# A two-layer trunk on one core: another order of the recurrence, and the one-token samples' new state made in the second feed-forward stage

## The chip, the cores and the metric

The kernel runs on one core of one Trainium2 chip. The metric is the device time of one execution in microseconds, from several runs. A profiled execution gives the trace. Engines are named as in the profile: PE is TensorE (matmuls, with their weight loads as PEld), DVE is VectorE, ACT is ScalarE, POOL is GpSimd, SP is SyncE, which here does nothing but issue DMAs.

## The reference

A trunk of two layers is run on a prompt of 256 tokens and, with its own states, on 8 samples of one token each. The kernel keeps them side by side: N = 264 columns, of which the first 256 are the prompt and the last 8 the samples. All is float32. A layer is:

```python
x = x + 0.5 * swiglu(rmsnorm(x, norm_ffn1), ffn1_w_in, ffn1_w_out)
h = rmsnorm(x, norm_mix); proj = h @ w_in
y_rwkv, shift, wkv = rwkv7_mix(...)      # 16 heads of 64
y_sc, sc_buf = short_conv_mix(...)
y_ssm, ssm_conv, ssm = mamba2_mix(...)
x = x + concatenate([y_rwkv, y_sc, y_ssm]) @ w_out
x = x + 0.5 * swiglu(rmsnorm(x, norm_ffn2), ffn2_w_in, ffn2_w_out)
```

The change is in rwkv7_mix. Per head, with a state S of 64 x 64, it does for each token

```python
Sa = einsum('bhij,bhj->bhi', S, -kk_t)
S = S * w_t[:, :, None, :] + Sa[..., None] * b_t[:, :, None, :] + v_t[..., None] * k_t[:, :, None, :]
y_t = einsum('bhij,bhj->bhi', S, r_t)
```

and then normalises y within each head (mean and variance over 64), scales it, adds a bonus and gates it. For a sample there is one token, an old state S read from memory (8 samples x 16 heads x 64 x 64) and a new state that is an output. For the prompt the kernel works in four chunks of 64 tokens, where each chunk needs the inverse of a triangular 64 x 64 matrix.

## The kernel before

A layer has two stages, "front" (first feed-forward, input projection, the two other mixers, the gates of this one) and "back" (the recurrence, the output product with w_out, the second feed-forward). Each engine has a list of its own, written out by hand, and works it in order; semaphores carry the dependences. So an instruction that waits holds all behind it on its engine.

**The recurrence.** Heads go in pairs: pair p is heads 2p and 2p+1, RT = 8 pairs. One loop over g = 0..9 overlaps three ages of pairs: in iteration g the youngest is g, then b = g-1, c = g-2 and p = g-3. For a pair the steps are:

- GpSimd `weigh` multiplies keys, queries and so on by the decays that ScalarE made (`decays`); TensorE `gram` makes the products of all tokens in a chunk; VectorE `mask` puts them into `products` (two operations); GpSimd makes `first` and VectorE `start` from them, the inverse at block size 1.
- Five levels (0 to 4) double the block size each. A level is: GpSimd `level` masks the products into `n_levels`; TensorE `level_t1` (16 small matmuls); ScalarE `t1_copy`; TensorE `level_u`; ScalarE `x_copy`; VectorE `turn_blocks`, a transpose. The last level ends with VectorE `finish`. A pair has its levels 0 and 1 in iteration g and 3 and 4 in the next; of level 2 GpSimd's and VectorE's part lies in iteration g, TensorE's at the start of the next. `order_of` numbers the levels over all pairs, and two buffers go round in that order.
- TensorE `turn` transposes keys and values, ScalarE `tokens` copies them. `gv`, `solve`, `transfer`, `own_outputs`, `own_states` and `chunk` 1 to 3 are TensorE's part of the chunk recurrence, ScalarE `rv_copy`, `uw_copy`, `state_copy`, `y_copy` the copies between them. `turn_final` and `final_copy` store the last state.
- The head norm of pair p: TensorE `mean_of` (ones within a head), VectorE `centre` subtracts the mean, ScalarE `square`, TensorE `variance_of`, ScalarE `variance`; VectorE `gated` scales. For five pairs together ScalarE then takes Ln and Exp at g = 8 (two table loads), for the last three after the loop.

**The samples.** At the front's end GpSimd gathers five vectors per sample (`vecs`: kk, decay, -b, k, r). TensorE turns them, SP writes them to a scratch in memory (`row_scratch`) and reads them back spread over 64 partitions, ten DMAs of 128 KB a pair (`load_row`). In iteration g VectorE does eight `step`s of 512 columns for pair b: state x kk, its sum, state x decay, (-b) x sum, two additions, state x r, its sum. The key term is GpSimd's `key_row`. SP stores the new state and loads that of pair b+2, each 256 KB in pieces of 256 bytes.

**The rest of back.** At the loop's end products with w_out begin (`short`, with the two other mixers' outputs, 24 matmuls each) between the recurrence's last steps, then come those with y. Weights are split into a high and a low part: ScalarE `split_hi`, VectorE or GpSimd `split_lo`, in rings of four halves; raw pieces of 1 MB come in a ring of three, SP's `ws.load(p)` waiting until the piece three before has been split. `Ffn` is the second feed-forward: 22 steps m of two halves, then 24 halves of the output product. In it GpSimd has work for the first two splits only.

The lines that the trace names: L2230 turn_x, L2218 level_t1 and level_u, L2196 turn, L2211 gram, L2264 gv, L2275 solve, L2296 and L2299 transfer, L2351 mean_of, L2355 variance_of on PE; L1822 t1_copy, L1829 x_copy, L1873 variance, L1927 and L1878 Ln and Exp, L209 split_hi, L1854 final_copy on ACT; L1750 level, L1772 first, L1758 key_row, L216 split_lo on POOL; L2026 mask, L2032 start, L2042 finish, L2063 to L2081 the steps on DVE; L232 to L234 the products with split weights.

## Time and profile before

| | us |
|---|---|
| median of 3 runs (1679.66 to 1681.52) | 1679.8 |
| the profiled execution | 1676.12 |
| its span in the trace | 1674.1 |
| busy in the span: PE, DVE, ACT, POOL | 1550.2, 1108.9, 881.6, 271.7 |
| mean granted clock of TensorE | 0.978 |

Layer 0's recurrence runs from about 440 to 610 us of the span, layer 1's from 1266 to 1430; behind each come the output product and the second feed-forward stage, in layer 1 from about 1475 to the end. Busy time says how much an engine did; what limits a stretch is seen where TensorE idles in it and in who released it. The granted clock is a share of 2.4 GHz, and only 0.50 and 1.00 occur for long.

### The profile page before, as it was taken

What the parts mean: (1) busy time and instruction counts of PE and PEld (TensorE: products, weight loads), DVE (VectorE), ACT (ScalarE), POOL (GpSimd) and SP (SyncE); (2) the same over time, 40 slices, a digit from 0 to 9 for tenths busy, and PEclk for the clock granted to TensorE, in tenths of its full rate; (3) what the DMA queues carried; (4) which work ended last, traced back from release to release, by engine and by line L of the source; (5) the groups of instructions that cost most, each with busy time, mean ns of one, the idle gap of its engine ahead of it and who ended that gap; (6) DMA issues with size and microseconds to landing.
All of it is one profiled execution on the core that took longest, in us unless ns stands there. A gap on an engine that the chain in (4) does not pass through costs nothing. (4 is left out here: it accounts for less than half of the span.)

```text
span 1674.1 us, 39220 instructions
## 1 busy us (share of the span) xinstructions
PE 1550.2 (93%) x16355; PEld 1463.3 (87%) x16355; DVE 1108.9 (66%) x1758; ACT 881.6 (53%) x1579; POOL 271.7 (16%) x259
## 2 busy tenths in 40 slices
PE   7999999999688889999999999999996898899997
PEld 6999999987577789999999999989775777899997
DVE  5565587785577757665475655968765777576654
ACT  5444464767355655444353444647673456554443
POOL 0000003001265621000000000030013665300000
PEclk9999999999889999999999999999997999999999
DMA  7555556371134545655454655643702446355552
GB/s 229 178 177 165 168 170 203 112 209 50 50 106 130 156 135 176 193 162 188 163 185 151 202 165 177 192 151 117 224 1 72 122 132 183 118 185 193 178 181 71
DMA packets 280642, 256.15 MB, mean 153 GB/s; under 512 B 48054, under 2 KB 268700, under 8 KB 280450
## 3 DMA queue, kind: packets, MB, share of 16 engines
q1 hardware_dynamic: 276698, 252.05, 48.7%
q8 instruction: 131, 2.15, 0.6%
q10 hardware_dynamic: 3768, 1.59, 0.4%
q14 instruction: 45, 0.37, 0.1%
HBM read 242.22 MB, written 11.38 MB: 151 GB/s over the span
## 5 line engine op out<-in xcount | busy, mean ns | idle before, releaser
L209 ACT ACTIVATE front_hi<-front_raw 128x1024 fp32r<-128x1024 f32 (+2 forms) x230 | 238.5, 1039 | 260.7 <-PE ps L234 249.5
L216 DVE TENSOR_TENSOR front_lo<-front_raw,front_hi 128x1024 fp32r<-128x1024 f32 (+1 forms) x210 | 252.3, 1201 | 109.4 <-ACT front_hi L209 108.4
L209 ACT ACTIVATE out_hi<-out_raw 128x1024 fp32r<-128x1024 f32 (+1 forms) x168 | 173.2, 1038 | 215.6 <-PE ps L234 201.3
L216 DVE TENSOR_TENSOR out_lo<-out_raw,out_hi 128x1024 fp32r<-128x1024 f32 (+1 forms) x148 | 179.7, 1214 | 106.2 <-ACT out_hi L209 105.4
L232 PE MATMUL ps<-front_h_hi,front_hi 128*128 128x264 f32 (+1 forms) x816 | 240.8, 295 | 4.9 <-DVE front_lo L216 3.3
L234 PE MATMUL ps<-front_h_hi,front_lo 128*128 128x264 f32 (+1 forms) x816 | 232.4, 285 | 0.0
L233 PE MATMUL ps<-front_h_lo,front_hi 128*128 128x264 f32 (+1 forms) x816 | 232.3, 285 | 0.0
L232 PE MATMUL ps<-ffn_h_hi,out_hi 128*128 128x264 f32 x704 | 200.4, 285 | 0.1
L233 PE MATMUL ps<-ffn_h_lo,out_hi 128*128 128x264 f32 x704 | 199.6, 284 | 0.0
L234 PE MATMUL ps<-ffn_h_hi,out_lo 128*128 128x264 f32 x704 | 199.6, 283 | 0.0
L232 PE MATMUL ps<-in_h_hi,front_hi 128*128 128x264 f32 x688 | 196.5, 286 | 0.0
L233 PE MATMUL ps<-in_h_lo,front_hi 128*128 128x264 f32 x688 | 195.6, 284 | 0.0
L234 PE MATMUL ps<-in_h_hi,front_lo 128*128 128x264 f32 x688 | 195.6, 284 | 0.0
L232 PEld LDWEIGHTS ps<-front_h_hi,front_hi 128*128 128x128 f32 (+1 forms) x816 | 153.7, 188 | 13.6 <-issue 11.9
L233 PEld LDWEIGHTS ps<-front_h_lo,front_hi 128*128 128x128 f32 (+1 forms) x816 | 153.7, 188 | 0.7
L234 PEld LDWEIGHTS ps<-front_h_hi,front_lo 128*128 128x128 f32 (+1 forms) x816 | 153.0, 188 | 0.1
L216 POOL TENSOR_TENSOR front_lo<-front_raw,front_hi 128x1024 fp32r<-128x1024 f32 (+1 forms) x20 | 49.8, 2490 | 543.0 <-ACT front_hi L209 543.0
L232 PEld LDWEIGHTS ps<-ffn_h_hi,out_hi 128*128 128x128 f32 x704 | 132.4, 188 | 0.6 <-ACT ffn_h_hi L283 0.5
L233 PEld LDWEIGHTS ps<-ffn_h_lo,out_hi 128*128 128x128 f32 x704 | 132.4, 188 | 0.1
L234 PEld LDWEIGHTS ps<-ffn_h_hi,out_lo 128*128 128x128 f32 x704 | 132.3, 188 | 0.0
L233 PEld LDWEIGHTS ps<-in_h_lo,front_hi 128*128 128x128 f32 x688 | 130.4, 190 | 0.1
L232 PEld LDWEIGHTS ps<-in_h_hi,front_hi 128*128 128x128 f32 x688 | 130.3, 189 | 0.1
(400 smaller groups left out, 3826.2 us busy)
## 6 DMA issues: line engine op xcount, KB each, us to landing
front_raw<-in_w_in SPq DMA_DIRECT2D x50, 1024.0 KB, 5.3
out_raw<-in_ffn_w_in SPq DMA_DIRECT2D x44, 1024.0 KB, 5.2
front_raw<-in_ffn_w_in SPq DMA_DIRECT2D x40, 1024.0 KB, 5.3
back_sample_rows<-row_scratch SPq DMA_DIRECT2D x160, 128.0 KB, 3.1
out_raw<-in_w_out SPq DMA_DIRECT2D x16, 1024.0 KB, 5.2
front_raw<-in_ffn_w_out SPq DMA_DIRECT2D x16, 896.0 KB, 4.7
out_raw<-in_ffn_w_out SPq DMA_DIRECT2D x16, 896.0 KB, 4.7
front_raw<-in_ffn_w_out SPq DMA_DIRECT2D x8, 1024.0 KB, 5.0
```

Of the source, the lines that this page charges most:

```text
L209: act.activation(self.hi[n % self.RING][:, 0:k, 0:w], self._raw(n), ACT.Copy).then_inc(self.hi_ready, 1)
L216: eng.tensor_tensor(self.lo[n % self.RING][:, 0:k, 0:w], self._raw(n), self.hi[n % self.RING][:, 0:k, 0:w].bitcast(F32), ALU.subtract).the ...
L232: pe.matmul(out, hi[:, j, 0:w], x_hi[:, j], start=start and j == 0, stop=False)
L233: pe.matmul(out, hi[:, j, 0:w], x_lo[:, j], start=False, stop=False)
L234: mm = pe.matmul(out, lo[:, j, 0:w], x_hi[:, j], start=False, stop=stop and j == k - 1)
```

## The change

It has two parts.

**The samples.** The output of a sample no longer needs its new state: y = S (decay x r) + (S kk) (-b . r) + v (k . r). So the vectors are now kk, decay x r (`REC`, a GpSimd product), decay, -b, k. In the recurrence VectorE does for each pair one product of 1024 columns (the old state with both rows) and one sum, and for every second pair three operations of 16 columns. The dot products within a head come from one matmul at the start. The state is not changed there; `SampleUpdate` makes it in the second feed-forward stage, which loads the old state a second time, with rows of three vectors. SP issues its DMAs behind the loads of pieces 10, 12, 15, 17, 20, ... (`place(n) + 8`), GpSimd makes two products a pair, VectorE three operations at the end of steps m = 2, 4, 7, 9, 12, 14, 17, 19. The next stage's first ScalarE operation (`act_hi(0)`) waits until all new states are stored, as the buffers lie where its output goes.

**The order.** Level 2 lies wholly in the next iteration now; `solve(b)` stands at the end of the iteration; `turn` comes ahead of turn_x. The centring is folded into the matrix of `mean_of` (`centre` = identity minus the mean within a head), so VectorE's `centre` goes and `square` and `gated` read PSUM. All five engines' lists in the loop are rearranged. TensorE's list of an iteration, first before, then after (a step whose pair is not in 0..7 is left out; `short` only at g = 8, 9):

```
t1(b,2) solve(c) turn_final(c-1) [9: short 2] turn_x(g) u(b,2) t1(g,0) turn(g,0) [8: short 0] transfer(c) mean(p)
  u(g,0) t1(b,3) turn(g,1) [9: short 3] own_outputs(c) u(b,3) t1(g,1) own_states(c) variance(p) [8: short 1]
  u(g,1) t1(b,4) chunk(c,1) gram(g+1) gv(b) chunk(c,2) u(b,4) chunk(c,3)
t1(b,2) turn_final(c-1) turn(g,0) turn(g,1) [8: short 0] u(b,2) turn_x(g) transfer(c) [9: short 2] t1(b,3) mean(p)
  u(b,3) t1(g,0) [9: short 3] own_outputs(c) own_states(c) u(g,0) t1(b,4) chunk(c,1) [8: short 1] gram(g+1)
  variance(p) u(b,4) t1(g,1) chunk(c,2) gv(b) u(g,1) chunk(c,3) solve(b)
```

ScalarE's, the same way (its copy after each of these, Ln and Exp with split_hi(2) at g = 8):

```
t1(b,2) uw(c) [9: split_hi 4, 5] final(c-1) x(g,0) x(b,3) decays(g+1) [8: Ln Exp split_hi 2] t1(g,0) tokens(g,0)
  x(g,1) t1(b,3) tokens(g,1) square(p) x(b,4) t1(g,1) state(c,0) [8: split_hi 3] variance(p) x(g,2) t1(b,4)
  state(c,1) rv(b) state(c,2) state(c,3) y(c) [7: split_hi 0, 1] [8: y_hi 0, 1]
uw(c) t1(b,2) [9: split_hi 4, 5] final(c-1) tokens(g,0) tokens(g,1) x(b,3) x(g,0) [8: Ln Exp split_hi 2] t1(b,3)
  square(p) x(b,4) [7: short_hi 0, 1] t1(g,0) state(c,0) x(g,1) decays(g+2) variance(p) t1(b,4) state(c,1)
  [7: short_hi 2, 3] [8: split_hi 3] t1(g,1) rv(b) state(c,2) x(g,2) state(c,3) y(c) [7: split_hi 0, 1] [8: y_hi 0, 1]
```

VectorE's:

```
start(g) turn(b,3) step 0 transfer(c) turn(g,1) step 1 centre(p) step 2 turn(b,4) step 3 gated(p) turn(g,2)
  2 bonus scalings (g < 4), 3 of y_short (g = 0), 5 (g = 1), step 4, mask(g+1) x2, step 5, finish(b) step 6 step 7
turn(b,2) start(g) transfer(c) turn(b,3) sample_products(b) gated(p) turn(b,4) sample_sums(b) turn(g,1)
  mask(g+1) x2, finish(b), sample_outputs (b odd), 2 bonus scalings (g < 4), 2 of y_short (g < 4)
```

The core of the rest of the diff, GpSimd's list in it (the indentation is cut):

```diff
+def sp(self, sp, n):
+  if n == 0:
+    sp.wait_ge(*self.free)
+  if n >= 2:
+    sp.wait_ge(self.done, 3 * (n - 1))
+    sp.dma_start(self.new[n - 2], self.state[(n - 2) % 3][:]).then_inc(self.stored[(n - 2) % 3], 16)
+  if n < RT:
+    for h in range(2):
+      sp.dma_start(self.rows[h * HS:(h + 1) * HS, n % 2].rearrange("p v b j -> p v (b j)"),
+             self.row_mem[DEC:KEY + 1, 2 * n + h].rearrange("v b j -> v (b j)").unsqueeze(0).to_broadcast([HS, 3, NS * HS])
+             ).then_inc(self.rows_in[n % 2], 16)
+    if n >= 3:
+      sp.wait_ge(self.stored[n % 3], 16 * (n // 3))
+    sp.dma_start(self.state[n % 3][:], self.old[n]).then_inc(self.state_in[n % 3], 16)
+def wait_stored(self, eng):
+  for i in range(3):
+    eng.wait_ge(self.stored[i], 16 * len(range(i, RT, 3)))
+def pool(self, pool):
+  for q in range(RT):
+    pool.wait_ge(self.rows_in[q % 2], 32 * (q // 2 + 1))
+    for i, x0 in ((1, self.env.sample_sums[:, q, 0]), (2, self.env.sample_v[:, q])):
+      row = self.rows[:, q % 2, i]
+      pool.tensor_tensor(row, row, x0.unsqueeze(2).to_broadcast([P, NS, HS]), ALU.mult).then_inc(self.products, 1)
+@staticmethod
+def place(n):
+  return 2 + 5 * n // 2
+def dve(self, dve, m):
+  q = next((n for n in range(RT) if self.place(n) == m), None)
+  if q is None:
+    return
+  st0 = self.state[q % 3]
+  dve.wait_ge(self.state_in[q % 3], 16 * (q // 3 + 1))
+  dve.wait_ge(self.rows_in[q % 2], 32 * (q // 2 + 1))
+  for i, op in ((0, ALU.mult), (1, ALU.add), (2, ALU.add)):
+    if i:
+      dve.wait_ge(self.products, 2 * q + i)
+      dve.wait_ge(self.done, 3 * q + i)
+    dve.tensor_tensor(st0[:], st0[:], self.rows[:, q % 2, i], op).then_inc(self.done, 1)
...
-for i, x0 in ((0, mix.kkn), (2, mix.nb), (3, k), (4, r)):
+for i, x0 in ((KK, mix.kkn), (MB, mix.nb), (KEY, k)):
   pool.tensor_copy(mix.vecs[:, :, i], x0[:, :, T:N]).then_inc(s("vecs"), 1)
+pool.wait_ge(s("decay_vec"), 1)
+pool.tensor_tensor(mix.vecs[:, :, REC], mix.vecs[:, :, DEC], r[:, :, T:N], ALU.mult).then_inc(s("vecs"), 1)
...
-order = [(g - 1, 2), (g, 0), (g - 1, 3), (g, 1), (g - 1, 4)]
+order = [(g - 1, 2), (g - 1, 3), (g, 0), (g - 1, 4), (g, 1)]
...
-  load_row(sp, 0, n)
-for m in range(RT):
-  if m == 6:
+for m in range(2):
+  load_rows(sp, m)
+for m in range(2, RT):
+  sp.wait_ge(s("sampled"), m - 1)
+  load_rows(sp, m)
+  sp.dma_start(state[:, m % 2], sin[m]).then_inc(s(f"state{m % 2}_in"), 16)
+  if m == RT - 1:
     sp.wait_ge(s("weighed"), 4 * (RT - 1))
     for p in range(3):
       ws.load(sp, p)
-  for n, used in ((KK, 1), (DEC, 3), (MB, 4), (KEY, 0), (REC, 7)):
...
 for p in range(3, len(pieces)):
   ws.load(sp, p)
+  for n in range(RT + 2):
+    if p == update.place(n) + 8:
+      update.sp(sp, n)
...
   pool.tensor_tensor(xt[:, g % 3], gm[:, g % 3, :, 0], first[:].unsqueeze(1).to_broadcast([P, 4, C]),
              ALU.mult).then_inc(s("first_done"), 1)
-  level(g, 0)
 if b >= 0:
+  level(b, 2)
   level(b, 3)
 if g + 1 < RT:
   weigh(g + 1)
 if g < RT:
-  level(g, 1)
-if g == RT - 1:
-  for q in range(3):
-    short_split_lo(q)
+  level(g, 0)
 if b >= 0:
   level(b, 4)
 if g == RT:
   ws.split_lo(pool, 2)
-if b >= 0:
-  key_row(b)
+if g < RT:
+  level(g, 1)
 if g == RT - 1:
-  short_split_lo(3)
-if g < RT:
-  level(g, 2)
-if g == RT - 1:
+  for q in range(4):
+    short_split_lo(q)
   ws.split_lo(pool, 0)
...
+  dve.wait_ge(s(f"state{m % 2}_in"), 16 * (m // 2 + 1))
+  dve.wait_ge(s(f"rows{m % 2}_in"), 32 * (m // 2 + 1))
+  if m:
+    dve.wait_ge(s("summed"), m)
+  dve.tensor_tensor(prod[:], state[:, m % 2].unsqueeze(1).to_broadcast([P, 2, NS, HS]), rows[:, m % 2],
+            ALU.mult).then_inc(s("sampled"), 1)
+def sample_sums(m):
+  dve.wait_ge(s("sampled"), m + 1)
+  dve.tensor_reduce(sums[:, m], prod[:], AX.X, ALU.add).then_inc(s("summed"), 1)
+def sample_outputs(m):
+  c = slice(m - 1, m + 1)
+  dve.wait_ge(s("summed"), m + 1)
+  dve.wait_ge(s("rec_done"), 1)
+  dve.wait_ge(s("v_read"), 2)
+  dve.tensor_tensor(b_rec[:, c], b_rec[:, c], sums[:, c, 0], ALU.mult).then_inc(s("sample_part"), 1)
+  dve.tensor_tensor(v_rec[:, c], v_rec[:, c], sums[:, c, 1], ALU.add).then_inc(s("sample_part"), 1)
+  dve.wait_ge(s("sample_part"), m + 1)
+  dve.tensor_tensor(r[:, c, T:N], b_rec[:, c], v_rec[:, c], ALU.add).then_inc(s("sample_out"), 1)
...
 def variance_of(p):
   pe.wait_ge(s("dev_sq"), p + 1)
+  pe.wait_ge(s("dev_gated"), p + 1)
   pe.matmul(ps[:, WB, 0:N], head, v[:, p], start=True, stop=True).then_inc(s("var_ps"), 1)
...
```

## Rows read from the trace of the kernel before

**Rows 1.** Stretches: start:end, us, busy PE, PEld, DVE, ACT, POOL, clock, DMA, GB/s.

```profile
1284.20:1288.90 4.70, 4.68 (x68) 4.24 (x70) 1.02 (x2) 2.25 (x6) 2.13 (x4) 0.50 0.02 3
...
1289.91:1293.00 3.09, 2.92 (x55) 2.30 (x55) 2.55 (x5) 2.66 (x7) 3.09 (x5) 1.00 0.15 52
...
1302.20:1303.40 1.20, 1.19 (x22) 1.19 (x24) 0.00 (x0) 0.12 (x2) 0.00 (x0) 0.50 0.44 156
...
1348.34:1363.31 14.97, 13.59 (x373) 11.56 (x373) 11.76 (x20) 8.66 (x25) 9.69 (x11) 1.00 0.45 128
...
1396.20:1399.20 3.00, 3.00 (x24) 2.94 (x24) 2.08 (x3) 2.75 (x3) 2.68 (x2) 1.00 0.24 69
...
1416.90:1418.00 1.10, 1.10 (x35) 1.00 (x35) 0.36 (x2) 0.00 (x0) 1.10 (x1) 1.00 0.98 349
...
1500.00:1598.00 98.00, 98.00 (x812) 98.00 (x812) 61.91 (x85) 46.52 (x69) 0.00 (x0) 1.00 0.55 179
```

**Rows 2.** Chain of waits: start us, duration us, engine, tile, line, count.

```profile
1302.21 1.12 PE ps L2230 x16
...
1317.75 0.68 PE ps L2230 x16
...
1345.93 0.81 DVE back_prod L2079
...
1346.77 0.69 DVE xs L2081
...
1347.45 0.84 DVE back_inverse_t L2032
...
1378.29 0.68 PE ps L2230 x16
```

**Rows 3.** TensorE's timeline: start, duration, line, tiles, count, idle before and releaser.

```profile
1284.22 1.12 PE L2230 MATMUL ps<-cst,back_inverse_t 64*64 64x64 f32 x16 [3.61 <-DVE back_inverse_t L2032]
...
1299.86 1.80 PE L2275 MATMUL ps<-back_gv_a,back_inverse_t 64*64 64x128 f32 x16 [3.76 <-DVE back_inverse_t L2042]
...
1348.34 0.68 PE L2230 MATMUL ps<-cst,back_inverse_t 64*64 64x64 f32 x16 [1.03 <-DVE back_inverse_t L2032]
...
1355.70 0.71 PE L2355 MATMUL ps<-xs,cst 128*128 128x264 f32 x2
...
1360.96 1.09 PE L2275 MATMUL ps<-back_gv_a,back_inverse_t 64*64 64x128 f32 x16 [0.29 <-DVE back_inverse_t L2042]
...
1393.40 0.62 PE L2218 MATMUL ps<-back_inverse,back_n_levels 64*64 64x64 f32 x15 [1.36 <-POOL back_n_levels L1750]
...
1403.40 0.62 PE L2218 MATMUL ps<-back_n_x,back_inverse_t 64*64 64x64 f32 x13 [1.70 <-ACT back_n_x L1822]
...
1416.89 0.46 PE L2296 MATMUL ps<-back_tok,back_u_w 64*64 64x64 f32 x16 [1.78 <-ACT back_final_state L1854]
```

**Rows 4.** Groups by line, 1318 to 1378 us: count, busy us, mean ns, idle.

```profile
L2071 DVE TENSOR_TENSOR back_outer<-back_sample_rows,back_sample_sa 128x512 f32<-128x512 f32 x4 | 4.5, 1137 | 0.0
...
L1758 POOL TENSOR_TENSOR back_outer<-back_sample_rows,xs 128x512 f32<-128x512 f32 x4 | 6.0, 1490 | 0.0
```

**Rows 5.** ScalarE's timeline, columns as before.

```profile
1356.45 0.39 ACT L1873 ACTIVATE xs<-ps 128x264 f32<-128x264 f32 x1 [0.30 <-PE ps L2355]
...
1396.82 1.28 ACT L1927 ACT_TABLE_LOAD   x1
...
1402.99 0.36 ACT L1822 ACTIVATE back_n_x<-ps 128x256 f32<-128x256 f32 x1
...
1487.67 1.06 ACT L209 ACTIVATE out_hi<-out_raw 128x1024 fp32r<-128x1024 f32 x1 [1.97 <-DMA out_raw<-in_ffn_w_in]
```

**Rows 6.** GpSimd's timeline, columns as before.

```profile
1393.69 2.36 POOL L216 TENSOR_TENSOR out_lo<-out_raw,out_hi 128x1024 fp32r<-128x1024 f32 x1 [0.55 <-ACT out_hi L209]
...
1396.01 2.87 POOL L1750 TENSOR_TENSOR back_n_levels<-back_products,cst 128x256 f32<-128x256 f32 x2
```

**Rows 7.** VectorE's timeline, columns as before.

```profile
1451.47 2.34 DVE L287 SCALAR_TENSOR_TENSOR ffn_h_lo<-x,cols,ffn_h_hi 128x264 fp32r<-128x264 f32 x1 [0.93 <-ACT ffn_h_hi L283]
```

More of the change, by code:

```diff
@@ L333, in act_hi @@
     def act_hi(self, act, k):
+        if k == 0 and self.update is not None:
+            self.update.wait_stored(act)
         act.wait_ge(self.x_ready, k + 1)
@@ L403, in pool @@
                 self.ws.split_lo(pool, n)
+        if self.update is not None:
+            self.update.pool(pool)
     def act(self, act):
@@ L474, in dve @@
                 self.side.dve(dve)
+            if self.update is not None:
+                self.update.dve(dve, m)
         hidden_lo(FT - 1)
@@ L533, in pe, with __init__ @@
                 self.following.pe_side(pe, i)
+class SampleUpdate:
+    def __init__(self, st, env, d, place, layer, free):
+        self.env, self.free, self.row_mem = env, free, d["row_scratch"]
+        self.old = d["state_rwkv_wkv"][layer].rearrange("b (m h) i j -> m (h i) b j", h=2)
+        self.new = d["s_wkv"][layer].rearrange("b (m h) i j -> m (h i) b j", h=2)
+        self.state, self.rows = [*env.upd_state, place("upd_state2", 75392, [P, NS, HS])], env.upd_rows
+        self.state_in = [st.sem(f"upd_state{i}_in") for i in range(3)]
+        self.rows_in = [st.sem(f"upd_rows{i}_in") for i in range(2)]
+        self.products, self.done = st.sem("upd_products"), st.sem("upd_done")
+        self.stored = [st.sem(f"upd_stored{i}") for i in range(3)]
+    def sp(self, sp, n):
[36 more added lines that the diff above has]
+            dve.tensor_tensor(st0[:], st0[:], self.rows[:, q % 2, i], op).then_inc(self.done, 1)
@@ L1929, in _ @@
                         ws.split_hi(act, 2)
+                    if 0 <= b < RT:
+                        t1_copy(b, 3)
+                    if p >= 0:
+                        square(p)
+                    if 0 <= b < RT:
+                        x_copy(b, 4)
+                    if g == RT - 1:
+                        short_split_hi(0)
+                        short_split_hi(1)
                     if g < RT:
@@ L2394, in _ @@
                         shift_turn(4)
-                    if c >= 0:
-                        solve(c)
                     if c >= 1:
                         turn_final(c - 1)
-                    if g == RT + 1:
-                        short(2)
-                    if g < RT:
-                        turn_x(g)
+                    if g and g < RT:
+                        turn(g, 0)
+                        turn(g, 1)
+                    if g == RT:
+                        short(0)
                     if 0 <= b < RT:
@@ L2442, in _ @@
                         chunk(c, 1)
+                    if g == RT:
+                        short(1)
                     if g + 1 < RT:
                         gram(g + 1)
+                    if p >= 0:
+                        variance_of(p)
                     if 0 <= b < RT:
-                        gv(b)
+                        level_u(b, 4)
+                    if g < RT:
+                        level_t1(g, 1)
                     if g == RT + 1:
```

289 lines of the change are left out of this document (121 added, 168 removed).

## The prediction

> **What bounds the kernel now.** I read the page first (shares of the engines), then the busy times by stretch, the chain of waits, and last the timelines of single engines in the two stages that the change touches. In the feed-forward stages TensorE is never idle and everything else has room: between 1500 and 1598 us it is busy 98.00 of 98.00 us, VectorE 61.91, GpSimd not at all, DMA at a share of 0.55 [rows 1]. Work added there is free so long as it has room. The recurrence (the "back" stage, once per layer, an iteration g for each pair of heads) is different. In its steady part an iteration takes 14.97 us, start of one turn_x (L2230) to the next [rows 1, 3], and the chain leaves TensorE at one place: VectorE ends an iteration with sample steps 6 and 7 (L2079, L2081), then makes start(g) (L2032), and only then turn_x starts [rows 2, 3]. TensorE waits 1.03 us for that and 0.29 us ahead of solve [rows 3]; the other 13.65 us it works through its own list, which is in order.
>
> The first iterations are worse. Turn_x(1) starts after 3.61 us of idle TensorE, solve(0) after 3.76 us [rows 3]. Behind both idle stretches the granted clock is 0.50, that is 1.2 GHz, until 1289.9 and 1303.4 us [rows 1]; solve(0) takes 1.80 us there, a later solve 1.09 [rows 3]. So iteration 1 takes 18.0 us and iteration 2 15.5 [rows 2].
>
> **Part 1: VectorE's sample work leaves the recurrence.** Eight steps of 512 columns per pair go, the longest 1.14 us [rows 4], in all about 6.3 us, and the centring with them (0.42). In their place stand one product and one sum of 1024 columns (1.2 us each, which a VectorE split of that size takes here; bounds 1.1 and 2.3, the longest row once and twice) and three tiny operations for every second pair. VectorE falls from 11.76 busy us of 14.97 [rows 1] to about 8, and nothing of the sample stands between finish(b) and start(g+1). GpSimd loses key_row. The waits of 1.03 and 0.29 us go. What is late next is not VectorE but ScalarE, below.
>
> **Part 2: iterations 0 to 2.** In iteration 0 the masks of pair 1 stand behind five scalings on VectorE, in iteration 1 finish(0) stands behind seven scalings, step 4, both masks and step 5. The new order puts masks and finish first. Of the 3.61 us idle about 1.5 stay (GpSimd must still make first and level 2 behind the masks), so 2.1 go; the 3.76 go whole; and without idle stretches of that length the two stretches at 1.2 GHz go, the first 5.7 us long and the second about 3.5, which cost 2.5 and 1.7. Against that GpSimd weighs pair 1 (four operations, 2.8 us) before level(0,0), which holds the first level back 1.3 us. Sum 2.1 + 3.8 + 4.2 - 1.3 = 8.8, taken as 9 us by the end of iteration 2. Bounds: 3 (only one idle stretch gone) and 11.
>
> **Part 3: iterations 3 to 6.** TensorE's 13.65 us shrink a little, by 0.4 (my estimate; between 0 and 0.7), as both turns now stand together and there are fewer changes between matmuls over 128 rows and over 64. New waits by the new lists: (a) variance_of(p) is followed on TensorE by level_u(b,4), whose t1_copy stands on ScalarE behind variance(p). After the 0.71 us of variance_of, which is issued for 0.65, ScalarE copies the variance (0.39) and then t1 (0.38) [rows 3, 5]: TensorE stands 0.85 us. Before, variance(p) had level_u(g,1) behind it, whose copy was done. (b) chunk(c,3) waits for state_copy(c,2), which now stands behind rv_copy: 0.35. (c) level_u(b,3) waits for a VectorE transpose behind transfer(c): 0.25. Period 13.65 - 0.4 + 1.45 = 14.7, less 0.1 of small overlaps: 14.6. Four iterations took 60.5 us (1317.75 to 1378.29, rows 2), they will take 58.4: 2.1 us gained. Bounds -2 and +4. By turn_x(7) the layer is 11 us ahead.
>
> **Part 4: iterations 7 to 9, where it is given back.** In iteration 7 GpSimd's list now is level(7,1), four short_split_lo, split_lo(0), and only then, in iteration 8, level(7,2). In the kernel before level(7,2) came ahead of split_lo(0). split_lo(0) waits for split_hi(0), which is at the end of ScalarE's iteration. Behind ScalarE's last copy of the iteration (13.5 us into it) come split_hi 1.0, split_lo 2.4 and the level 0.9 or more [rows 6]: TensorE can begin level_t1(7,2) at 18.0, and its last work, solve(6), ends at 13.9. **It idles 4.1 us.** Then: short(0), 3.0 us [rows 1], now stands ahead of level_u(7,2). ScalarE's block of Ln, Exp and split_hi(2) starts behind x_copy(7,3), which needs that level_u, and holds t1_copy(7,3) for 6.2 us (1396.82 to 1402.99, rows 5). Before, short(0) ran under this block and TensorE waited 1.70 [rows 3]. Now it has only transfer, one level_t1 and mean_of, 1.8 us, and **idles 5.3 us** at level_u(7,3). With 0.85 of (a) twice and the small waits, idle time between solve(5) and the end of solve(7) rises from 7.5 us (34.9 us long, waits of 1.36 and 1.70 among it, rows 3) to about 12.3: a loss of 4.7.
>
> On top, the clock. In this trace idle stretches of 3.61 and 3.76 us were followed by 1.2 GHz for 5.7 and 3.5 us, one of 1.78 was not (1.00 in the stretch behind it, rows 1, 3). Both new stretches are longer than those that lost it. Price by the same rows: 2.5 us for the usual length, a little more where full products of short(0) fall in it: 5.3 for both.
>
> The Trainium skill ("TensorE: Matmul & The Clock Gate", section "Why this matters for your kernels") says to leave no long gaps between bursts of matmuls, or the engine falls back to its lower clock. It speaks against this change twice, for the gaps before level_t1(7,2) and level_u(7,3); by the rule alone, the price would be the same as by the rows here, and the trace agrees with it.
>
> In iteration 9 short(2) no longer covers ScalarE's split_hi(4), split_hi(5) and final_copy ahead of transfer(7), where TensorE waited 1.78 us with the cover [rows 3]: about 3.0 us of idle, net loss 1.2. Whether that loses the clock a third time (another 2.5), lies between the rows of 1.78 and 3.61 us; I take no. The missing centring gives 0.45 at mean_of(7). Making the record vector on GpSimd instead of copying it costs 0.2 at the stage's start.
>
> Per layer: 9 + 2.1 - 4.7 - 5.3 - 1.2 + 0.45 - 0.2 = 0.15 us gained.
>
> **Part 5: the update in the second feed-forward stage.** 24 VectorE operations of 512 columns, 0.68 each, three to every 2.5 steps (14.45 us), 16 GpSimd ones of 1.5 like key_row now [rows 4]. DMA: the rows come as two of 384 KB and the state as 256 KB in and out, 1.28 MB each 14.45 us, 89 GB/s. The stretch 1348 to 1363 moved 128 GB/s at a share of 0.45, so this is about 0.31, on 0.55: 0.86 [rows 1]. SP's queue issues four more DMAs (0.4 to 0.6 us each) and waits for done two updates back; from the ring's timing it stands at most 2.6 us, behind a weight load whose successor is due 8.7 us later. VectorE would be at 63% + 14%. Beside GpSimd work it can be held: an operation of 0.49 us lasted 2.34 beside a GpSimd split [rows 7]. If it is held for all 3 us of GpSimd's products it is at 98% and still under. The ring holds a half 5.7 us before TensorE needs it, even where a load was late (1487.67, rows 5). TensorE hides all of it; I take 0.4 us a layer for the first update, whose wait for the end of the output product and whose megabyte stand ahead of the load of piece 11. Bounds 0 and 4. The Trainium skill ("GPSIMD Engine Reference", section "Specifications") says GpSimd's SBUF interfaces are shared with VectorE, with contention where VectorE has two SBUF inputs. Each of the 24 updates is such an operation; by the rule the worst case of 98% would be the usual one, and TensorE would still hide it.
>
> **Sum.** Both layers: -0.3 + 0.8 = +0.5 us. The profiled execution took 1676.12 (span 1674.1); the median of the runs is 1679.8, 3.7 above it, and I let the difference stand. Forecast 1680.5 us.
>
> **Rivals.** *B, the early gain stays.* The clock doesn't fall in iteration 8, as TensorE's gaps there come out shorter: 5.3 us a layer more, 1670. For it: the gaps are sums of many small terms. Against: one is longer than both stretches that cost the clock here by 0.4 us, the other by 1.5. *C, the recurrence gets slower.* Iterations 1 and 2 turn out bound by the level chain (matmul, copy, matmul, copy, transpose), which the new list runs with no other pair's levels between, so that only about 6 of 9 us come, and transfer(7)'s 3.0 us gap loses the clock a third time: 5 to 6 us a layer less, 1689. It decides from the point where that gap costs the clock, somewhere between the 1.78 us that did not and the 3.61 us that did. For it: two gaps of nearly that length cost it. Against: the steady iterations have slack everywhere but on TensorE. *D, the feed-forward stage is no longer hidden.* An odd weight load falls behind the update's DMAs in several updates and the ring runs dry: 1 us for each of eight, 1686 to 1690. Against: the spacing of 8.7 us. *E, the removed waits are all that matters*, and TensorE's new list has no waits: 13.3 us an iteration, 1.3 x 4 more a layer, 1669; it has the variance row against it. E is counted with B.
>
> **Chances.** Forecast (net within 3 us of nothing to 5 slower) 0.40, B with E 0.32, C 0.22, D 0.06. A change under 0.2% (3.4 us) can't be told from none. Of the forecast 0.03 falls on faster, 0.24 on the same, 0.13 on slower; of B 0.02, of C 0.01 on the same. Faster 0.33, same 0.27, slower 0.40. Range 1667 to 1692; the forecast's own is 1677 to 1685.
>
> **What would show it.** Right: the steady turn_x period at 14.4 to 14.8 us; a TensorE wait of 0.8 us behind L2355's successor for ScalarE's n_x copy; no 3.6 us idle in iterations 0 and 1; level_t1(7,2) waiting some 4 us for GpSimd's level, level_u(7,3) some 5 us for ScalarE, with a granted clock of 0.50 behind each; TensorE 100% busy through the feed-forward stage with DMA at 0.8 to 0.9. Wrong: turn_x(7) less than 8 us earlier than now after the stage's start, clock 1.00 behind the two gaps, or TensorE idle in the feed-forward stage.

## The result, and the profile after

The changed kernel takes 1698.14 us (median of 4 runs, 1697.39 to 1703.31), the one before, run beside it, 1679.73. The ratio is 1.0119, with a 95% interval of 1.0093 to 1.0145: slower, and outside both the forecast's own range (1677 to 1685) and the whole range given (1667 to 1692). The profiled execution is the run of 1703.31 us, some 5 us above its fellows, so where a size matters I read it off several kernels below.

The first two rows are of the page after (idle time in front of ScalarE's splits, by releaser, that is by what ended the idle time; issues of DMAs with their microseconds to landing), the third is the same page's row on the rows of the samples:

```profile
L212 ACT ACTIVATE out_hi<-out_raw 128x1024 fp32r<-128x1024 f32 (+1 forms) x168 | 172.4, 1034 | 178.8 <-DMA out_raw<-in_ffn_w_in 89.6
...
out_raw<-in_ffn_w_in SPq DMA_DIRECT2D x44, 1024.0 KB, 8.5
...
upd_rows<-row_scratch SPq DMA_DIRECT2D x32, 384.0 KB, 8.0
```

A weight load of the second feed-forward stage lands 8.5 us after its issue, and ScalarE waits 89.6 us for such loads. Stretches of the changed kernel, columns as in [rows 1]: iterations 0 to 2 of layer 1, iterations 3 to 6, one steady iteration, five short stretches at the recurrence's start and end, and the 22 steps of the second feed-forward stage in layer 1:

```profile
1286.31:1325.71 39.40, 31.67 (x792) 28.38 (x794) 26.67 (x42) 22.36 (x61) 25.39 (x33) 0.96 0.37 86
1325.71:1381.31 55.60, 50.98 (x1499) 45.13 (x1497) 34.64 (x62) 31.83 (x96) 26.48 (x37) 1.00 0.35 90
1339.54:1353.45 13.91, 12.77 (x379) 11.29 (x377) 8.53 (x16) 8.28 (x26) 7.47 (x11) 1.00 0.27 62
...
1289.50:1292.50 3.00, 2.95 (x26) 2.46 (x26) 0.00 (x0) 2.82 (x8) 0.00 (x0) 0.50 1.05 242
...
1388.80:1398.80 10.00, 9.24 (x145) 8.36 (x147) 0.86 (x2) 4.57 (x14) 2.56 (x2) 0.51 0.01 3
1403.90:1408.50 4.60, 4.60 (x33) 4.48 (x34) 0.00 (x0) 0.61 (x2) 1.35 (x2) 0.50 0.70 235
1417.60:1421.00 3.40, 3.40 (x96) 3.40 (x98) 2.04 (x3) 0.88 (x3) 2.08 (x1) 0.50 0.00 0
...
1433.90:1436.00 2.10, 2.10 (x13) 2.08 (x10) 1.89 (x3) 0.00 (x0) 0.14 (x1) 0.50 0.13 23
...
1488.60:1624.30 135.70, 130.82 (x1058) 128.66 (x1057) 99.98 (x139) 63.96 (x91) 20.66 (x16) 1.00 0.94 250
```

The steady iteration is 13.91 us long, where [rows 1] had 14.97, and VectorE is busy 8.53 us of it, where it had 11.76. The feed-forward stage's DMA share went from 0.55 to 0.94, and TensorE, which had been busy all the time there, is idle for 4.9 us. TensorE's timeline (start, duration, line, tiles, count, idle before and releaser) has these idle stretches in layer 1's iterations 3 to 9 and in the feed-forward stage:

```profile
1347.58 0.68 PE L2263 MATMUL ps<-back_inverse_t,back_n_x 64*64 64x64 f32 x16 [0.76 <-ACT back_n_x L1874]
...
1388.77 0.59 PE L2367 MATMUL ps<-back_u_w,back_tok 64*64 64x64 f32 x11 [2.89 <-issue]
...
1403.88 1.12 PE L2263 MATMUL ps<-back_inverse,back_n_levels 64*64 64x64 f32 x16 [4.54 <-POOL back_n_levels L1814]
...
1417.56 1.00 PE L2263 MATMUL ps<-back_n_x,back_inverse_t 64*64 64x64 f32 x13 [5.17 <-ACT back_n_x L1874]
...
1432.86 0.71 PE L2341 MATMUL ps<-back_tok,back_u_w 64*64 64x64 f32 x16 [2.82 <-ACT back_final_state L1906]
...
1520.40 0.39 PE L235 MATMUL ps<-ffn_h_hi,out_hi 128*128 128x264 f32 x1 [1.12 <-DVE ffn_inner L464]
```

Against [rows 3]: the 3.61 and 3.76 us of the first iterations are gone; at the end stand 4.54 us for GpSimd's level, 5.17 for ScalarE's block of Ln and Exp and 2.82 ahead of transfer(7), where there were 1.70 and 1.78; and one of 2.89 us has no releaser at all (`issue`: no semaphore in the profile explains it).

From starts of turn_x, solve, the end of mean_of(7) and the first and last matmul of the 22 steps, in us, layer 0 / layer 1 (rec is from gram(0) to the end of mean_of(7)); the runs below it are told of in the next section:

| profiled run | gram(0) to turn_x(3) | to turn_x(7) | to solve(7) | to mean_of(7)'s end | rec | 22 steps |
|---|---|---|---|---|---|---|
| before | 51.6 / 51.6 | 62.3 / 60.5 | 32.8 / 32.6 | 17.2 / 17.1 | 163.9 / 161.8 | 129.0 / 129.0 |
| after | 45.8 / 44.1 | 60.1 / 55.6 | 44.5 / 47.5 | 20.0 / 19.9 | 170.3 / 167.1 | 139.0 / 135.9 |
| no_update | 44.8 / 44.3 | 61.6 / 55.6 | 44.0 / 43.1 | 19.9 / 19.8 | 170.2 / 162.8 | 129.2 / 129.2 |
| big_pieces | 46.0 / 44.7 | 61.5 / 55.6 | 44.8 / 43.7 | 19.9 / 19.7 | 172.2 / 163.8 | 131.0 / 135.4 |
| dma_only | 46.1 / 44.8 | 62.6 / 55.6 | 44.9 / 43.5 | 20.0 / 19.7 | 173.5 / 163.6 | 129.2 / 131.6 |
| ops_only | 45.3 / 44.8 | 61.0 / 56.0 | 43.2 / 46.3 | 19.8 / 19.8 | 169.4 / 166.9 | 131.7 / 133.5 |
| after_later | 48.5 / 44.4 | 61.6 / 55.6 | 42.9 / 46.3 | 19.8 / 19.8 | 172.7 / 166.0 | 131.0 / 130.3 |
| after_spread_loads | 45.5 / 44.8 | 60.9 / 55.6 | 40.1 / 42.8 | 21.1 / 19.9 | 167.7 / 163.1 | 139.2 / 138.7 |
| levels_first | 45.3 / 44.4 | 59.5 / 55.6 | 41.3 / 41.0 | 19.9 / 19.8 | 165.9 / 160.8 | 134.8 / 139.0 |
| tail_order | 46.0 / 44.4 | 60.6 / 55.6 | 36.0 / 38.8 | 17.4 / 17.4 | 160.0 / 156.1 | 133.5 / 134.7 |
| tail2 | 45.7 / 44.3 | 62.3 / 55.6 | 35.2 / 37.7 | 17.4 / 17.4 | 160.5 / 155.0 | 134.6 / 135.4 |
| spread_ops | 46.0 / 44.3 | 61.1 / 55.6 | 35.4 / 34.6 | 17.4 / 17.4 | 159.8 / 152.0 | 132.4 / 134.9 |
| one_later | 45.9 / 44.4 | 62.3 / 56.0 | 35.4 / 36.4 | 17.4 / 17.4 | 161.1 / 154.2 | 132.0 / 129.7 |
| loads_spread | 45.7 / 46.6 | 64.1 / 55.7 | 33.1 / 31.0 | 17.5 / 17.4 | 160.4 / 150.7 | 139.3 / 139.5 |
| all_three | 45.6 / 44.4 | 61.2 / 56.0 | 32.5 / 33.1 | 17.5 / 17.4 | 156.8 / 150.8 | 131.7 / 129.9 |
| inline | 47.0 / 45.5 | 63.0 / 58.5 | 36.3 / 39.0 | 17.4 / 17.4 | 163.7 / 160.4 | 129.1 / 129.2 |
| inline_spread_loads | 46.7 / 46.0 | 66.8 / 60.1 | 34.4 / 36.5 | 17.4 / 17.4 | 165.3 / 160.0 | 129.2 / 129.2 |

So in the profiled runs the recurrence lost 6.4 and 5.3 us, and the feed-forward stage 10.0 and 6.9. That is 28.6 us; all the rest of the kernel gained 1.2, which leaves the 27.4 between the spans (1701.5 and 1674.1).

### The profile page after: what moved, and what is told of

Read it like the earlier page. It is cut to its first block and busy times, and to the rows that moved or that the text cites. A ratio compares the mean times of both kernels' runs of the same rounds, so it can differ in the third digit from the quotient of the medians.

```text
span 1701.5 us, 39114 instructions
## 1 busy us (share of the span) xinstructions
PE 1551.1 (91%) x16359; PEld 1469.7 (86%) x16359; DVE 1083.3 (64%) x1728; ACT 875.0 (51%) x1579; POOL 278.8 (16%) x275
## 5 line engine op out<-in xcount | busy, mean ns | idle before, releaser
L212 ACT ACTIVATE out_hi<-out_raw 128x1024 fp32r<-128x1024 f32 (+1 forms) x168 | 172.4, 1034 | 178.8 <-DMA out_raw<-in_ffn_w_in 89.6
L219 DVE TENSOR_TENSOR out_lo<-out_raw,out_hi 128x1024 fp32r<-128x1024 f32 (+1 forms) x148 | 184.0, 1243 | 124.2 <-ACT out_hi L212 123.5
L235 PE MATMUL ps<-ffn_h_hi,out_hi 128*128 128x264 f32 x704 | 202.9, 288 | 10.9 <-DVE ffn_inner L464 9.2
L235 PEld LDWEIGHTS ps<-front_h_hi,front_hi 128*128 128x128 f32 (+1 forms) x816 | 152.4, 187 | 13.1 <-issue 12.3
L235 PEld LDWEIGHTS ps<-ffn_h_hi,out_hi 128*128 128x128 f32 x704 | 133.1, 189 | 14.6 <-DVE ffn_inner L464 11.5
L235 PEld LDWEIGHTS ps<-in_h_hi,front_hi 128*128 128x128 f32 x688 | 131.0, 190 | 0.1
```

The costliest lines, as they stand in the source:

```text
L212: act.activation(self.hi[n % self.RING][:, 0:k, 0:w], self._raw(n), ACT.Copy).then_inc(self.hi_ready, 1)
L219: eng.tensor_tensor(self.lo[n % self.RING][:, 0:k, 0:w], self._raw(n), self.hi[n % self.RING][:, 0:k, 0:w].bitcast(F32), ALU.subtract).the ...
L235: pe.matmul(out, hi[:, j, 0:w], x_hi[:, j], start=start and j == 0, stop=False)
```

## The experiments

Each median is of 5 to 12 runs; the ratio is to the kernel before, run between them (its medians there 1678.09 to 1679.25).

**What the update costs at all: no_update.** `SampleUpdate`'s methods return at once, so the samples' new state is left out.

> The changed kernel with the samples' new state left out (it is neither loaded, made nor stored). Account from the trace: the 22 steps of the second feed-forward stage took 138.7 and 135.7 us in the changed kernel and 128.8 in both layers before. If the update is the whole cause there, both come back to 128.8 and the time falls by 17 us in all, to about 1681. Rival (the recurrence's own loss also reaches into that stage, for instance by a late first load): the steps stay above 131 us and less than 12 us come back, 1686 or more.

Measured 1685.85 us, ratio 1.0043 (1.0028 to 1.0058). The steps come back to 129.2 us in both layers, so the whole of that stage's loss is the update's and the rival is out. But in time it is 12.3 us, not the 17 I took from one profile, whose run was a long one. The other 7.3 us against the kernel before are the new order's. (The two make 19.6 and not the 18.4 between the first medians, as the kernel before was 1.2 us faster when it ran beside this one.)

**The order's end: levels_first and tail_order.** Edits in GpSimd's list, then in TensorE's:

```diff
   for q in range(4): short_split_lo(q)
+  level(g, 2)                     # g = 7, no longer in iteration 8
+  level(g, 3)
   ws.split_lo(pool, 0)
---- tail_order also:
-  if g == RT: short(0)
   if 0 <= b < RT: level_u(b, 2)
+  if g == RT: short(0)
   if g < RT: turn_x(g)
+  if g == RT + 1: short(2)
   if c >= 0: transfer(c)
-  if g == RT + 1: short(2)
```

> The changed kernel, with GpSimd's level(7,2) and level(7,3) ahead of split_lo(0). Theory: TensorE's idle 4.5 to 4.9 us ahead of level_t1(7,2) is GpSimd's list alone; level_t1(7,2) then follows solve(6) at once, but short(0) needs split_lo(0) and stands about 2.5 us, so 2 us a layer come back and the clock perhaps as well (up to 2.5 a layer): 1689 to 1694. Rival (split_hi on ScalarE is what all wait for, the level is not the last): level_t1(7,2) still starts 4 us behind solve(6), 1697 or more.

> As levels_first, and on TensorE level_u(7,2) ahead of short(0), short(2) ahead of transfer(7), as in the kernel before. Theory: the order of iterations 7 to 9 alone gives the early gain back. Idle of 4.5 becomes 2.5, that of 5.2 ahead of level_u(7,3) about 2.2 (ScalarE's Ln and Exp then run under short(0)), that of 2.8 ahead of transfer(7) about 0.5 or nothing: 7.5 us a layer of waits and 2 to 5 us of clock, so 19 to 25 us in all: 1673 to 1679. Rival (the chain of ScalarE copies of pair 7 is the bound whatever TensorE does between): less than 10 us, 1688 or more.

Measured 1690.88, ratio 1.0080 (1.0065 to 1.0094), and 1676.83, ratio 0.9997 (0.9981 to 1.0013): both inside what was expected. Both fences are of TensorE in layer 1. In levels_first (first fence) the wait has moved to short(0), which needs split_lo(0), and is 2.58 us long, as forecast; the wait for ScalarE's block is still 5.17. In tail_order (second fence) that one is 0.64, but level_u(7,2) waits 4.02 us for a transpose on VectorE, which I had missed: it stands behind VectorE's split_lo(1).

```profile
1391.85 0.36 PE L235 MATMUL ps<-short_hi,out_hi 128*128 128x264 f32 x1 [2.58 <-POOL out_lo L219]
...
1402.66 1.00 PE L2265 MATMUL ps<-back_n_x,back_inverse_t 64*64 64x64 f32 x13 [5.17 <-ACT back_n_x L1876]
```

```profile
1386.32 0.68 PE L2265 MATMUL ps<-back_n_x,back_inverse_t 64*64 64x64 f32 x16 [4.02 <-DVE back_inverse_t L2094]
...
1394.02 0.62 PE L2265 MATMUL ps<-back_n_x,back_inverse_t 64*64 64x64 f32 x13 [0.64 <-ACT back_n_x L1876]
```

So the order of iterations 7 to 9 alone, with all else of the change kept, is worth 21.3 us and wipes out the slowdown.

**The transpose: tail2.** As tail_order, with `turn_blocks(7, 2)` ahead of `ws.split_lo(dve, 1)`.

> As tail_order, and VectorE's turn_blocks(7,2) ahead of split_lo(1), behind which it stood: in tail_order TensorE idles 4.0 us ahead of level_u(7,2) for that transpose. Theory: the idle stretch falls to about 2.4 us (ScalarE's split_hi(0), split_hi(1) and uw_copy(6) stay ahead of its t1_copy), 1.6 us a layer, and if the clock no longer falls behind it another 1 to 2: 1669 to 1674 against tail_order's 1676.8. Rival (ScalarE's own list is the later of the two by then): 1676 or more.

Measured 1677.26, ratio 0.9985 (0.9972 to 0.9999): the rival, and not to be told from tail_order. The wait fell to 1.69 us (about 2.4 forecast), but 2.06 us (with 0.64 before) now stand at level_u(7,3); the chain of ScalarE's copies gives only 1 us a layer.

**What in the update costs: big_pieces, dma_only, ops_only.** big_pieces views the old and the new state as 128 pieces of 2 KB. dma_only makes SP's store wait for the old state's landing and leaves out the GpSimd and VectorE operations. ops_only loads rows for pairs 0 and 1 and states for pairs 0 to 2, stores nothing, and runs all 40 operations.

> The changed kernel, with the update's old and new state moved as 128 pieces of 2 KB a DMA in place of 1024 of 256 bytes; the same bytes and DMAs, so the new state is made from the wrong elements of the old. Theory: the small pieces make the DMA engines the bound (200 GB/s while they move, 350 with weights alone), so the DMA share falls from 0.95 to under 0.85 in the stage, the load of a piece lands in under 7 us instead of 8.5, and at least two thirds of the 17 us come back: 1687 or less. Rival (the bytes themselves, or SP's queue that waits for VectorE's last update, or the added VectorE and GpSimd operations): steps stay at 135 to 139 us, 1694 or more.

> The changed kernel with the update's DMAs alone: rows and old states are loaded and stored again as they are, and neither GpSimd nor VectorE makes anything of them. Theory (the DMA engines are the bound of the second feed-forward stage): its 22 steps take 134 to 139 us, as in the changed kernel, against 129.2 without the update; time 1693 to 1698. Rival (the added operations, or SP's wait for VectorE's last one): 131 us or less a layer and 1689 or less.

> The changed kernel with the update's 24 VectorE and 16 GpSimd operations, but with rows and old states loaded for the first pairs alone, and no new state stored. Theory (DMA): the 22 steps take 129 to 130 us a layer, time 1685 to 1688, as without the update (1685.9). Rival (VectorE is held beside GpSimd's products and its splits come late): 133 us or more a layer and 1693 or more.

Measured 1692.70, ratio 1.0085 (1.0066 to 1.0103); 1689.93, ratio 1.0064 (1.0047 to 1.0081); and 1692.72, ratio 1.0083 (1.0059 to 1.0107). All three times lie between what the theory and what the rival gave. The steps say more. My theory that the DMA engines alone are the bound fell: the DMAs alone cost 0 and 2.4 us of steps although their share was the highest of all, 0.97 (the fence below, the steps of layer 1 in dma_only). The operations alone cost 2.5 and 4.3, nearly all of it in steps 4 and 6; both together cost 7 to 10. Bigger pieces gave 5.4 us: the share fell from 0.94 to 0.88 only, SP waited for VectorE even longer (10.9 us in layer 1, against 9.6 below), and yet the steps took 131.0 and 135.4 us. So SP's wait, told of next, seems to cost what it does together with slow loads and not by itself; this rests on one profile.

```profile
1479.90:1611.50 131.60, 129.46 (x1058) 128.60 (x1057) 79.22 (x114) 64.33 (x92) 0.00 (x0) 1.00 0.97 253
```

What dma_only and ops_only both lack is a link from VectorE to SP. SP's waits in the 22 steps of layer 1 of the changed kernel (total us, times, longest):

```profile
SPq L193 <- DVE out_lo L219: 80.4, 19, 10.9
SPq L565 <- DVE upd_state L601: 9.6, 4, 3.6
SPq L196 <- ACT out_hi L212: 3.5, 9, 1.7
SPq L568 <- PE ps L237: 2.9, 1, 2.9
```

The update of pair n is issued behind the load of the weights for step place(n), which the ring lets go about five steps ahead. It begins with a wait for VectorE's last operation of pair n-2, five steps earlier: that is just being done. And in VectorE's list (changed kernel) three operations stand in a lump at a step's end, ahead of the work that TensorE needs:

```profile
1515.90 0.43 DVE L468 TENSOR_TENSOR ffn_hid_lo<-ffn_inner,ffn_hid_hi 128x264 fp32r<-128x264 f32 x1
1516.25 2.28 DVE L601 TENSOR_TENSOR upd_state<-upd_state,upd_rows 128x512 f32<-128x512 f32 x3
1518.44 0.43 DVE L456 TENSOR_TENSOR ffn_gate_normed<-ps,ffn_rs 128x264 f32<-128x264 f32 x1
1518.79 1.22 DVE L219 TENSOR_TENSOR out_lo<-out_raw,out_hi 128x1024 fp32r<-128x1024 f32 x1
1519.92 0.42 DVE L464 TENSOR_TENSOR ffn_inner<-ffn_silu_gate,ps 128x264 f32<-128x264 f32 x1
```

The lump makes 6.0 us of VectorE work (2 x 1.22, 3 x 0.43, 2.28) in a step that lasts 5.8 us without the update. The next three runs take the lump, SP's wait and a third thing apart, on top of tail2.

**Lump, SP's wait, and the fetch: spread_ops, one_later, loads_spread, all_three.**

```diff
---- spread_ops: VectorE's operation 0 of pair q at step place(q) - 1, operations 1 and 2 at place(q)
---- one_later, in SP's list:
-  if p == update.place(n) + 8: update.sp(sp, n)
+  if p == update.place(n) + 9: update.sp(sp, n)
---- loads_spread, in SP's list, iteration 6:
   for p in range(3):
+    if p: sp.wait_ge(s("t1_ps"), order_of[(6, 1) if p == 1 else (7, 0)] + 1)
     ws.load(sp, p)
```

> As tail2, with VectorE's first operation of each update one step earlier than the other two (so one at the end of a step, two at the end of the next, where three stood in a lump). Neither the DMAs alone (0 and 2.4 us) nor the operations alone (2.5 and 4.3) cost what both together do (5 to 10 us a layer). Theory A (the lump: 2.28 us behind 3.72 us of VectorE's own work makes 6.0 us in a step of 5.78, so VectorE can't catch up what a late load cost it): with 5.24 us at most the 22 steps take 130 to 132 us instead of 134.6 and 135.4; 1669 to 1673 against tail2's 1677.3. Theory B (SP stands 1 to 3 us at VectorE's last operation of the update before and holds the weight load behind it): nothing changes, 134 us or more, 1675 or more.

> As tail2, with every update's DMAs one weight load later in SP's queue, so that VectorE's last operation of the update two back, for which SP waits, lies a step behind. Theory B (SP's wait, 9.1 us in four times, one of 4.4 ahead of the first): the wait is gone, the 22 steps take 130 to 132 us, 1669 to 1673. Theory A (VectorE's lump) or plain DMA load: SP's wait goes, the steps stay at 134 or more, 1675 or more.

> As tail2, with the first three weight loads of the output product (3 MB, issued at once in iteration 6) spread: the second waits for level_t1(6,1), the third for level_t1(7,0). Theory: TensorE's gap of 2.9 us in iteration 7 of layer 1, which no semaphore explains, is its instruction fetch standing behind these 3 MB (the DMA share is over 1.0 for 10 us, and the 16 KB fetch starts where they end); spread, the gap falls under 1 us in layer 1, and with it the 1.2 GHz stretch that follows: 3 to 5 us, 1672 to 1674. Rival (the fetch is late for another reason, such as a jump of the instruction buffer): the gap of over 2 us stays and the time is 1676 or more.

> The three together. If A, B and the late instruction fetch are separate costs, their gains add: 1660 to 1668, faster than both kernels by 0.6% or more. If A and B are one loop (VectorE late, so SP late, so the next load late), either alone breaks it and both together give little more than one: 1667 to 1672.

| | median, us | ratio (95%) |
|---|---|---|
| spread_ops | 1670.93 | 0.9952 (0.9938 to 0.9966) |
| one_later | 1669.31 | 0.9942 (0.9927 to 0.9957) |
| loads_spread | 1675.10 | 0.9968 (0.9952 to 0.9984) |
| all_three | 1660.72 | 0.9889 (0.9873 to 0.9904) |

one_later: SP's wait for VectorE is gone (first fence, its waits in layer 1), and the steps take 132.0 and 129.7 us with the same bytes and the same VectorE work as before the edit (second fence, the steps of layer 1: DMA share still 0.93, VectorE still 99.91 us busy). Theory B holds, and one load later takes 8.0 us off tail2's median.

spread_ops came out at theory A's time, 6.3 us below tail2. Its profiled steps do not bear A out: they lost a third as much as in one_later (134.6 to 132.4, 135.4 to 134.9), within the scatter of this stage (last section), and SP still waited 7.6 us in layer 1 (9.1 in tail2). The rest of the difference between the two profiled runs is in the recurrence, which the edit does not touch: behind the gap of iteration 7 of layer 1 the clock stood at 0.50 for 10.2 us in tail2's run, for 3.4 in this one. all_three's steps (131.7, 129.9) are no better than one_later's, so in the profiled runs the lump mattered only while SP waited for its end. But the medians add up as for separate costs: 6.3, 8.0 and 2.2 us below tail2 make 16.5, and all_three is 16.5 below. Whether the lump costs anything of its own stays open; no run spreads it with SP's wait gone and the loads left together.

```profile
SPq L193 <- DVE out_lo L219: 81.3, 20, 8.5
SPq L196 <- ACT out_hi L212: 3.1, 10, 0.9
SPq L568 <- PE ps L237: 0.6, 1, 0.6
```

```profile
1461.00:1590.70 129.70, 129.25 (x1059) 128.34 (x1058) 99.91 (x137) 64.38 (x91) 24.22 (x16) 1.00 0.93 255
```

loads_spread: the gap of iteration 7 that had no releaser (2.89 in layer 1 in tail2 too) is gone in layer 1, and turn_x(7) to solve(7) falls from 35.2 and 37.7 to 33.1 and 31.0. The steps took 139 us in the profiled run, which gave it back there; that run was the longest of its twelve (1681.67, median 1675.10), so how typical these steps are isn't known. all_three, which has all three edits, is 1.1% faster than the kernel before and 2.2% faster than the changed one.

**The same two edits on the changed kernel itself: after_later, after_spread_loads.**

> The changed kernel with the update's DMAs one weight load later in SP's queue and nothing else. Theory (SP's wait for VectorE's last update is most of the feed-forward stage's loss): the 22 steps take 130 to 132 us a layer instead of 139 and 136, the recurrence stays as it is, 1687 to 1690 (without the update at all it was 1685.9). Rival (it helped only because the recurrence's end was repaired): 134 us or more a layer and 1694 or more.

> The changed kernel with the three first weight loads of the output product spread over iterations 6 and 7 and nothing else. Theory (instruction fetch behind 3 MB): the gap of 2.9 us in iteration 7 of layer 1 falls under 1 us and the clock does not fall there, so turn_x(7) to solve(7) shortens from 47 us to 41 to 43 in layer 1 and by 1 to 3 us in layer 0; 1691 to 1695. Rival (the longer idle stretches ahead of the level and the Ln/Exp block swallow it): 1697 or more, turn_x(7) to solve(7) still over 45.

after_later measured 1689.45, ratio 1.0066 (1.0052 to 1.0080), steps 131.0 and 130.3: as expected, SP's wait is worth 8.7 of the change's 18.4 us. after_spread_loads measured 1698.00, ratio 1.0115 (1.0097 to 1.0133): the rival's time. The largest gap without releaser in iteration 7 of layer 1 is 1.09 us, and turn_x(7) to solve(7) is 40.1 and 42.8, the shortest of the seven kernels with that list (in layer 1 by 0.3 us only), so something of the mechanism is there; the whole time did not move, and again the steps are at the top of their spread (139.2, 138.7). Both kernels with the loads spread and SP's wait in had such steps, so the one may bring on the other; no run tells, and it stays open.

**The update left in the recurrence, in the new order: inline, inline_spread_loads.** Both on top of tail2: one set of five rows as in the kernel before, `decay_state(b)` ahead of the masks, GpSimd's two products behind level(g,1), `add_terms(c)` behind start(g). The second has the three loads apart.

> As tail2, but the samples' new state is made in the recurrence, in the new order: rows are single-buffered, GpSimd makes its two products behind level(g,1), VectorE decays the state ahead of the masks and adds the two terms behind start of the next iteration, the old state is loaded once. Theory: the recurrence has room for it (VectorE 8.5 and GpSimd 7.5 busy us of a period of 13.9, DMA share 0.27), so the period stays at 14 to 14.5 us while the feed-forward stage's 5 to 10 us a layer come back: 1658 to 1668. Rival (GpSimd's products hold first(g+1) or VectorE's additions hold start, and the period goes to 15 us or more): 1672 or more, so that moving the update out was worth its price.

> As inline (the update in the recurrence, in the new order), with the three weight loads one an iteration's part apart. Theory: the recurrence has the room, inline lost to the late fetch (3.4 us, and the clock behind it): 1664 to 1669, between one_later and all_three. Rival (VectorE and GpSimd are too full there): the iterations 5 and 6 stay over 15 us, 1673 or more.

Measured 1677.35, ratio 0.9994 (0.9982 to 1.0006), and 1674.83, ratio 0.9981 (0.9971 to 0.9991). The steps are back at 129.2, but the recurrence costs 3.2 and 5.4 us more than in tail2, and spreading the loads gave 2.5. In time the rival holds, in the period for the most part: iterations 3 to 6 take 63.0 / 58.5 and 66.8 / 60.1 us instead of tail2's 62.3 / 55.6, so 14.6 to 16.7 an iteration. The update in the recurrence costs as much as the update moved out with SP's wait (1677.35 and 1677.26); moved out without that wait it is 8 us better (1669.31). So moving it out pays, but only with the right place in SP's queue.

## Why the prediction was wrong

**Part 1, right.** VectorE at 8.53 us an iteration (about 8 forecast).

**Part 2, oversized.** 9 us forecast, 5.8 and 7.5 measured. The 3.61 and 3.76 us idle stretches went. What stayed is GpSimd's chain: 1.41 us ahead of turn_x(0), then 1.82 us ahead of level_t1(0,0) because four weighings of pair 1 stand ahead of level(0,0), and 1.64 in iteration 1, ahead of level_t1(0,2). And the clock was not saved entirely: after the first two the granted clock was 0.50 from 1289.5 to 1292.5.

**Part 3, right in kind, too small in layer 1.** The wait of variance(p) was 0.76 us (0.85 forecast), (b) and (c) together 0.22 (0.60), and TensorE's busy time fell by 0.8, from 13.59 to 12.77 (0.4 forecast; no run shows which of the rearrangements did it). Period 13.91 in layer 1: 4.9 us gained, not 2.1. In layer 0 TensorE has gaps of about 0.7 us without releaser in most of these iterations (last section): 2.2 gained.

**Part 4, the waits right, the clock wrong.** Idle stretches of 4.54, 5.17 and 2.82 us, forecast 4.1, 5.3 and 3.0. levels_first, tail_order and their rows showed each releaser to be the one named. The step that failed is "whether that loses the clock a third time ... I take no": it did, 0.50 behind the 2.82 us, and from solve(7) to the end of mean_of(7) it is 19.9 us where it was 17.1 (forecast loss 0.75, measured 2.8, in both layers). Not foreseen at all is the gap of 2.89 us in iteration 7 of layer 1, after which the clock stood at 0.51 for 10 us. With it turn_x(7) to solve(7) lost 14.9 us in layer 1 and 11.7 in layer 0, where I had 10.0. The idle stretches of 2.82, 2.89, 4.54 and 5.17 us were each followed by a stretch at 1.2 GHz, so for these the trace agrees with what the prediction cites from the Trainium skill ("TensorE: Matmul & The Clock Gate", section "Why this matters for your kernels"); I had applied it to two of the four. But the rows of single stretches, between which I placed the price, do not decide it by length: in layer 0 a stretch of 1.74 us in iteration 7 was followed by 0.50 as well (552.3 to 555.5 us), while in the kernel before one of 2.37 us at the same place was not (1.00 from 564.7 to 568.0), a row that I had not read.

Per layer I had +0.15 for the recurrence; it was -6.4 and -5.3. That is rival C in size (5 to 6 us a layer less) and in kind, a smaller early gain and a third loss of the clock at transfer(7)'s gap; in layer 1 it also took the gap of iteration 7, which C did not have, against 2.8 us more gained in the steady iterations.

**Part 5, the step that failed most.** "TensorE hides all of it; I take 0.4 us a layer", with SP standing "at most 2.6 us, behind a weight load whose successor is due 8.7 us later". The DMA share (0.86 forecast, 0.94), VectorE's busy time and the bytes were near; none of them was the bound, as dma_only at 0.97 shows. SP stood 9.6 us in four waits, up to 3.6, the loads behind it landed in 8.5 us instead of 5.2 (in dma_only, without this wait, in 8.4, so the landing time is the DMA load's doing), and the work it waited for was itself late when the loads were. The worst case for VectorE did not come: its 48 operations on the state took 0.69 us in the median, 1.53 at most, and it was busy 99.98 of 135.70 us. I had priced three parties apart, each with slack on average, and not the loop through all of them. Rival D described it (1 us for each of eight updates) and got a chance of 0.06. By the medians of after, no_update and before the stage cost 12.3 us and the order 7.3; by after_later 8.7 of the 12.3 are SP's place in the queue.

C and D at once lay outside the range, since I had taken them as alternatives, though nothing in one excludes the other. Both were also added up too low: C's 5 to 6 us a layer make 1690.5 to 1692.5, not 1689, and D's eight updates in each of two layers make 16 us and 1696.5, not 1686 to 1690. (The forecast itself is 1679.8 + 0.5 = 1680.3, printed as 1680.5.)

## What to carry to other kernels

A queue instruction that waits for another engine's work prices everything behind it: place it where the awaited work is a full step old, and check this by counting steps, not by shares of busy time. When an order is changed in a software pipeline, go through its last two iterations separately, for every engine; here a gain of 8 and 12 us a layer was lost by a few placements at the end. Independent rivals can both be true, and the range has to hold their sum.
